# Normalisation and input projection merged into one stage, with the value differences formed in it

## What is computed

```python
h = layer_norm(x, ln0_g, ln0_b)
proj = jnp.einsum('btd,dc->btc', h, w_in[l])
qa, ka, va, qb, kb, vb, gate = jnp.split(proj, split_at, axis=-1)
ya = dilated_mixture(heads_a(qa), heads_a(ka), heads_a(va), rel_bias)
yb = stick_breaking(heads_b(qb), heads_b(kb), heads_b(vb))
y = jnp.concatenate([ya, yb], axis=-1) * jax.nn.silu(gate)
out = jnp.einsum('btc,cd->btd', y, w_out[l]) + b_out[l]
h = layer_norm(DEEPNORM_ALPHA * h + out, ln_g[l], ln_b[l])
```

## Time and profile before

| what | us |
|---|---|
| median of 3 runs | 2041.08 (2038.07 to 2041.69) |
| span of the profiled execution | 2037.5 |
| TensorE matmul busy | 1769.6 (87%) |
| VectorE busy | 1250.8 (61%) |
| ScalarE busy | 781.5 (38%) |
| GpSimd busy | 341.2 (17%) |

### The profile page before, as it was taken

How to read it: one execution, slowest core, us unless ns; L and a number is a source line. 1 busy time by engine, 2 the same in 40 slices (tenths; PEclk the granted TensorE clock), 3 DMA queues, 4 the chain that set the end, 5 groups by cost and what they waited for, 6 DMA issues and landing times. The chain is left out here.

```text
span 2037.5 us, 29563 instructions
## 1 busy us (share of the span) xinstructions
PE 1769.6 (87%) x9134; PEld 1473.7 (72%) x9134; DVE 1250.8 (61%) x2303; ACT 781.5 (38%) x1927; POOL 341.2 (17%) x222
## 2 busy tenths in 40 slices
PE   4688999999999999487887788788998999959886
PEld 3566888888887878365666566567998989947775
DVE  8402122121122321699999999995776676768998
ACT  5301111111110010365565565565886776830000
POOL 4100000000000000312212211310222222206554
PEclk8798999999999999789899999997999999969998
DMA  5396233331121431804413440435897978363331
GB/s 169 56 108 167 113 141 117 121 137 62 62 93 55 114 88 41 193 10 91 93 31 67 90 89 14 87 67 131 190 205 184 197 191 192 95 214 138 124 124 72
DMA packets 224187, 230.92 MB, mean 113 GB/s; under 512 B 126996, under 2 KB 187412, under 8 KB 215357
## 3 DMA queue, kind: packets, MB, share of 16 engines
q1 hardware_dynamic: 170540, 162.09, 31.9%
q10 hardware_dynamic: 51424, 62.93, 8.6%
q0 software_dynamic: 2112, 4.73, 3.3%
HBM read 145.03 MB, written 84.67 MB: 113 GB/s over the span
## 5 line engine op out<-in xcount | busy, mean ns | idle before, releaser
L411 PE MATMUL proj<-h_hi,w_hi 128*128 128x512 f32 x1024 | 403.3, 394 | 33.0 <-DVE w_lo L497 29.6
L411 PE MATMUL proj<-h_hi,w_lo 128*128 128x512 f32 x1024 | 400.6, 391 | 0.0
L411 PE MATMUL proj<-h_lo,w_hi 128*128 128x512 f32 x1024 | 400.2, 391 | 0.0
L805 PE MATMUL wt_ps<-ident,W 128*128 128x128 f32 x1088 | 189.3, 292 | 97.3 <-DVE WT_lo L908 95.4
L899 DVE TENSOR_TENSOR_SCAN W<-w,W,zeros 128x512 f32<-128x512 f32 x192 | 266.5, 1388 | 0.0
L805 PEld LDWEIGHTS wt_ps<-ident,W 128*128 128x128 f32 x1088 | 129.8, 146 | 179.7 <-DVE WT_lo L908 105.7
L858 ACT ACTIVATE WT_hi<-wt_ps 128x512 fp32r<-128x512 f32 (+1 forms) x320 | 171.0, 534 | 209.4 <-PE o_ps L825 205.3
L411 PEld LDWEIGHTS proj<-h_hi,w_hi 128*128 128x128 f32 x1024 | 193.5, 189 | 73.9 <-issue 34.6
L521 DVE TENSOR_TENSOR st_lo<-proj,st_hi 128x512 fp32r<-128x512 f32 x64 | 44.0, 691 | 299.7 <-ACT st_hi L469 250.8
L411 PEld LDWEIGHTS proj<-h_hi,w_lo 128*128 128x128 f32 x1024 | 193.2, 189 | 40.7
L411 PEld LDWEIGHTS proj<-h_lo,w_hi 128*128 128x128 f32 x1024 | 193.5, 189 | 39.7
(11 more groups left out here) (116 smaller groups left out, 3138.1 us busy)
## 6 DMA issues: line engine op xcount, KB each, us to landing
w_raw<-in_w_tiles SPq DMA_DIRECT2D x32, 512.0 KB, 3.4
qk_hi_d<-st_hi ACTq DMA_DIRECT2D x16, 1024.0 KB, 3.9
qk_lo_d<-st_lo ACTq DMA_DIRECT2D x16, 1024.0 KB, 6.8
va<-va_d SPq DMA_DIRECT2D x32, 512.0 KB, 10.6
moved<-move_d SPq DMA_DIRECT2D x16, 528.0 KB, 4.2
x_sb<-in_x SPq DMA_DIRECT2D x16, 512.0 KB, 3.7
gate_d<-st_lo ACTq DMA_DIRECT2D x8, 1024.0 KB, 3.9
q_hi<-qk_hi_d SPq DMA_DIRECT2D x16, 512.0 KB, 10.0
```

The costliest lines, as they stand in the source:

```text
L411: last = pe.matmul(acc[s % 4][:], w[j][:, k, :], h[:, k, cols], start=(n == 0), stop=(n == len(passes) - 1))
L805: last = pe.transpose(t_ps[n % 4][:, i * P:(i + 1) * P], W[(turn_index(u) + i) % W_SLOTS][:, j * P:(j + 1) * P], ident[:])
```

## The change

`norm_phase` and `projection_phase` become one block, `front_phase`. A "step" s is one column block k of one chunk g of 512 positions (s = 8g + k, 32 steps). In each step TensorE does the four transposes of step s + 2 and then 9 matmuls: the three products of block k for each of the first `LEAD` = 3 weight tiles. So the first 3 tiles (12 of the 128 groups) are projected while the rows are being normalised; the other 29 tiles (116 groups) follow as before. Further:

- x is normalised in place, in 8 slots. ScalarE writes gain and bias back into the transposes' PSUM bank (`ln_tp`), then copies the high part out; VectorE subtracts from the bank. `ln_tp` has two banks.
- The high part of the weights moves from VectorE to ScalarE (`high_w`); one `w_raw` buffer stands where there were two.
- Results are stored group by group (512 positions), from two staging tiles `st`, and SP issues the stores, between its loads.
- The three DMAs of the bias tables move from GpSimd to SP; their sources lie in `st`, so the first two results (`first(0)`, `first(1)`) wait for `toe_stored`.
- For values of B, ScalarE copies the result shifted by one column (`shifted`), VectorE subtracts before the transposes, and the differences are stored split, as `dv_d` (rows of 512 bytes for each head). The block ends are collected in `vend`, transposed once and stored as `vend_d`.
- In `stick_phase` the values' three loads become two, and `differences` is gone.
- The order of the weight tiles changes.

```diff
+    LEAD = 3
...
+    X_SLOTS, W_SLOTS, ST_SLOTS, ACC_SLOTS, T_SLOTS, V_SLOTS = 8, 3, 2, 4, 2, 2
+        @block.sync
...
+            for c in range(3):
+                sp.wait_ge(toe_out, c + 1)
+                src = st[c % 2][0:HEADS, (c // 2) * CH:(c // 2) * CH + TOE]
+                sp.dma_start(toe_d[c], src.unsqueeze(1).broadcast_to([HEADS, P, TOE])).then_inc(toe_stored, 16)
+            load_w(LEAD)
+            for g in range(1, NCH):
+                if g + 1 < NCH:
+                    for n in range(QB * (g + 1), QB * (g + 2)):
+                        load_x(n)
+                for n in range(LEAD * (g - 1), LEAD * g):
+                    store(n)
...
+        @block.tensor
...
+            for s in range(STEPS):
+                g, k = divmod(s, KD)
+                pe.wait_ge(lo_done, s + 1)
+                for t in range(LEAD):
+...
+                    products(n, k, k == KD - 1)
+                if s + T_SLOTS < STEPS:
+                    transposes(s + T_SLOTS)
...
+        @block.scalar
...
+            def first(n):
+                kind = KIND[n]
+                if n >= ST_SLOTS:
+                    act.wait_ge(st_stored[n % ST_SLOTS], stored_by(n - ST_SLOTS))
+                else:
+                    act.wait_ge(toe_stored, 16 * 3)
+...
+            for s in range(STEPS):
+                g, k = divmod(s, KD)
+                normed(s)
+                if s in (0, 1):
+                    high_w(s + 1)
...
+                if g > 0 and k == 0:
+                    for n in range(LEAD * (g - 1), LEAD * g):
+                        first(n)
+            high_w(LEAD)
...
+        @block.vector
...
+            for s in range(STEPS):
+                g, k = divmod(s, KD)
+                low_h(s)
+                if s in (0, 1):
+                    low_w(s + 1)
+                if g > 0 and k == 0:
+                    for n in range(LEAD * (g - 1), LEAD * g):
+                        second(n)
+                if g + 1 < NCH and k < QB:
+                    moments(QB * (g + 1) + k)
+                if g + 1 < NCH and 0 < k <= QB:
+                    normalise(QB * (g + 1) + k - 1)
-            pool.wait_ge(w_split, 2 + TILES)
-            for c in range(3):
-                pool.dma_start(toe_d[c], toe[:, c, :].unsqueeze(1).broadcast_to([HEADS, P, TOE])) \
-                    .then_inc(toe_stored, 16)
-            def differences(it, par):
-    ...
-                pool.tensor_tensor(v_diff[:], v_prev[par][:], v_cur[par][:], ALU.subtract).then_inc(dv_step, 1)
```

More of the change, by code:

```diff
@@ L156, in wait_high @@
[L156 to L168, removed]
+        full_done, hi_done, lo_done = m.sem("h_full_done"), m.sem("h_hi_done"), m.sem("h_lo_done")
@@ new lines, in _ @@
+            for n in range(4):
+                load_x(n)
+            load_w(0)
+            load_x(4)
+            load_x(5)
+            load_w(1)
+            load_x(6)
+            load_x(7)
+            load_w(2)
+            sp.wait_ge(rb_set, 2)
+            sp.dma_start(rb[0:N_BUCKETS, :], rel_bias).then_inc(rb_loaded, 16)
+            for c in range(3):
+                where = vt[c] if c < 2 else tin[0]
+                sp.dma_start(where[0:N_BUCKETS + 1, 0:TOE], onehot[:, c * TOE:(c + 1) * TOE]) \
+                    .then_inc(oh_loaded, 16)
@@ new lines, in _ @@
+            for n in range(LEAD * (NCH - 1), LEAD * NCH):
+                store(n)
+            for n in range(MAIN, len(GROUPS)):
+                t, ch = GROUPS[n]
+                if ch == 1 and t + 1 < W_TILES:
+                    load_w(t + 1)
+                if n > MAIN:
+                    store(n - 1)
+                if n == VB_LAST + 3:
+                    sp.wait_ge(vend_copied, 1)
+                    for a in range(2):
+                        sp.dma_start(vend_d[:, :, a, :],
+                                     vend_t[a * TB:(a + 1) * TB, :].rearrange("b (h d) -> b h d", h=HEADS)) \
+                            .then_inc(vend_stored, 16)
@@ L182, in _ @@
+            store(len(GROUPS) - 1)
+            for slot in range(ST_SLOTS):
+                sp.wait_ge(st_stored[slot], stored_by(len(GROUPS) - ST_SLOTS + slot))
+            sp.wait_ge(vend_stored, 16 * 2)
         @block.gpsimd
@@ L191, in _ @@
                 .then_inc(ident_step, 1)
-            pool.wait_ge(ident_step, 2)
-            def deviation(n):
+            for n in range(TB):
                 pool.wait_ge(mv_done, n + 1)
@@ L245, in _ @@
[L245 to L271, removed]
-                    for c in range(3):
-                        last = pe.matmul(toe_ps[c][0:HEADS, 0:TOE], rb[:], oh[:, c * TOE:(c + 1) * TOE],
-                                         start=True, stop=True)
-                    last.then_inc(toe_mm, 1)
@@ L277, in _ @@
[L277 to L303, removed]
@@ L549 @@
+            low_w(LEAD)
+            for n in range(LEAD * (NCH - 1), LEAD * NCH):
+                second(n)
+            for n in range(MAIN, len(GROUPS)):
+                t, ch = GROUPS[n]
+                if ch == 2 and t + 1 < W_TILES:
+                    low_w(t + 1)
+                if n in V_INDEX:
+                    out_of_acc(n)
+                if n - 1 in V_INDEX:
+                    second(n - 1)
+                if n not in V_INDEX:
+                    second(n)
 class HeadTiles:
```

566 lines of the change are left out of this document (285 added, 281 removed).

## The result

The changed kernel takes 2054.63 us in the median of 5 runs (2049.63 to 2057.91), the kernel before 2041.08 in 5 runs taken with them: a ratio of 1.0076, 95% interval 1.0057 to 1.0096. That is slower by 0.8%, more than the noise of the runs. The forecast was 2039, with faster as the likeliest outcome (0.41); the time lies inside the forecast range of 2005 to 2062, but on the side that got 0.31. The profiled execution spans 2050.1 us against 2037.5, so the profile has 12.6 of the 13.6 us to explain.

The account below looks back on a forecast made before the run. The prediction took TensorE to bound the projection from 200 us on and VectorE the stick phase. The stick phase starting 36.6 us later, less 38 gained, gave -1.4 on 2041.1: 2039.7, rounded to 2039; range 2005 to 2062.

Parts of the forecast that it names:

- the stick phase's gain: Stick phase without GpSimd's differences: 33.4 us from scans, 3 from the load, 1.5 from three scans at the start, sum 38.
- The rest of the merged part: From the tables' landing at 140 to the merged part's end at 208.7: 5 + 20.4 + 22.4 + 19.5 + 1.4 us.
- the chain-bound rival: Merged part's steps limited by the chain through two `ln_tp` banks: 3.5 us a step, +19, time 2058; chance 0.15.
- The stall: Merged part: TensorE stands still from 58 to 145, 87 us, while ScalarE's first results wait for the tables.
- The rival of quick tables: Tables on SP's queue done by about 70 us, the stall shrinking by 70, time 1969; chance 0.12.
- The rival of 28 GB/s: Eight engines carry the tables at 3.5 GB/s each, taking 169 us, 73 more, time 2112; chance 0.05.
- The 1.6 us of start: Start allowance for the tables' DMAs on SP's queue, in 42 + 1.6 + 96 = 140 for their landing.
- The prediction's own sign of being wrong: Merged part: the prediction is wrong if steps take over 2.9 us; it had 2.67 in the mean.
- The old stall: Kernel before, 100 to 150 us: TensorE's wait of 29.6 us in two pieces on the weights' split, said to go.
- check of 816.7: Kernel before: 74.7, TensorE's groups, transposes, 29.6 of wait and 2.6 of slow matmuls, against last transposes at 816.23.

Follow-up runs that it names:

- e3: Changed kernel with the third result copy and subtraction of each chunk moved three steps later: 2031.4 us, 0.9960 of the kernel before.
- e7: Changed kernel with tables computed on 128 partitions but stored from eight of them, 16 apart: 2004.2 us, 0.9836 of the kernel before.
- e8: Changed kernel with four copies of each head's row and tables stored from eight partitions, 4 apart: 1981.1 us, 0.9712 of the kernel before.
- e4: Changed kernel with tables computed on 128 partitions and stored from all 128: 1972.1 us, 0.9666 of the kernel before.
- e1: Changed kernel with bias tables staged in tiles only the value groups need, still on SP's queue: 2049.7 us, 1.0058 of the kernel before.
- e2: Changed kernel with bias tables staged in tiles only the value groups need and sent from GpSimd's queue: 2024.4 us, 0.9945 of the kernel before.
- b1: Kernel before, without value differences on GpSimd, values loaded straight into the operands: 1999.8 us, 0.9806 of the unedited kernel before.

## Why the prediction was off

The sum, term by term, in us:

| term | predicted | measured |
|---|---|---|
| the tables' DMAs are issued at | 42 | 41.0 |
| they land at | 140 | 137.7 |
| from there to the end of the merged part (224.4) | 68.7 | 86.7 (e3: 67.2) |
| from there to the start of the stick phase (875.7) | 651.3 | 651.3 |
| the stick phase's gain | 38 | 38.7 |
| change of the span | -1.4 | +12.6 |

**The step that failed** is "The rest of the merged part": 68.7 us predicted, 86.7 measured. It put the wait for a free slot of `st` at nothing there. It charged the three results with "three copies on ScalarE (0.6 each, overlapped to 1.5)" after the landing and with "one of 4.0 where the three results come in" in each chunk, as work alone. The third copy is not only work: it reuses the slot of the first, whose store has only just been issued. In the three places inside this stretch the wait took 7.5, 5.5 and 3.3 us, 16.3 in all, and TensorE came back from each at a lower clock, an estimated 3.3 us more than behind the long stall alone. e3 took these waits away, and the stretch came out at 67.2 (from the landing at 136.38 to 203.57), 1.5 under the prediction's 68.7. The fourth wait, 3.8, lies behind the stretch and costs TensorE little: it is busy 5.51 of the 6 us from 224 to 230. (The 68.7 has a slip of its own: 19.5 for chunk 3 is less than eight steps of its 2.55, 20.4.) The prediction did look at this buffer, and only in the long phase: "Stores of 256 or 512 KB a group have two groups, 10.9 us, until their staging tile is wanted." That holds for the 116 groups of 5.4 us and is confirmed there (651.3). In the merged part three results come at once, so the cover is not two groups but none.

That the time still lies in the range is luck. The range reached up to 2062 for the sake of the chain-bound rival, whose 2058 is nearer to 2054.6 than my own number, but for a reason that did not hold (below).

**The stall was right, and so was its size.** The tables moved at 50 GB/s from SP's queue as from GpSimd's, and landed 2.3 us before the forecast. The source was the limit: e7 shows it by changing only where the eight partitions lie (51 to 103 GB/s), and e8 and e4 fit (202 and 364). The rival of quick tables (0.12) was wrong: 0.51 MB in 10 us from SP's queue in e1, 0.50 from GpSimd's in e2. The rival of 28 GB/s was wrong too, since half the engines (a share of 0.44) carried 50. The prediction put the stall down to `first(0)`'s wait alone and let the queue matter only for x and the weights; e1 shows that the place in the queue makes the stall without that wait, by the store behind the tables. The 1.6 us of start in the sum stand in no row and no run shows them; from the issue at 41.0 to the landing at 137.7 are 96.7 us, and 4.73 MB at 50 GB/s leave some 2 of them.

**Steps.** The prediction's own sign of being wrong, steps over 2.9 in the merged part, came true in the mean: 23 steps took 86.7 - 5 - 1.4 = 80.3 us, 3.5 each. That is the chain-bound rival's figure, but the rival did not hold: a step without moments takes 2.52 where TensorE's own work was put at 2.55, and in e3 the low parts of steps with moments start at 163.11, 165.78 and 168.49, 2.7 apart, the 2.72 that the prediction took from the earlier trace rows. The mean is made of such steps and three waits.

**The old stall.** The prediction said "the old stall of 29.6 goes". 18.6 was there to go. Its check of 816.7 counted the 11.03 twice, since 74.7 already held it, so the check agreed by accident: without it the sum is 805.7, 10.5 short. The trace of the kernel before places most of these: TensorE is idle for 5.0 us between 600 and 816, where the value groups are; it does 29 matmuls in 8.59 busy us from 160 to 170, at a clock of 0.73, some 2 us more than at full clock; and a group takes 5.44 us (22 of them between the copies at 500.92 and 620.60), not 5.42. The forecast does not use that sum, so its number is not touched.

**Stick phase.** 33.4 for the scans beside GpSimd and up to 2.4 for the three at the start; b1 has 36.4 for all of them, the changed kernel 36.8. 38 in all against 38.7. Without the differences the scans' median stays (1.267 and 1.268) and only the long ones go. These runs show that the differences cause the stretch, not by what means. In the pair of rows that the prediction shows, the excess (3.44 - 0.68 = 2.76) is longer than the whole `v_diff` instruction (2.36); it fits only with the gate product that GpSimd runs just ahead of it (L755, 941.52 to 942.84), from the scan's start at 942.28 to the end of L736 at 945.17.

## What to carry to other kernels

When an asynchronous store reads from a ring of staging tiles, count for each stage how many results come in a burst and how long the store holds a slot: two slots were ample for one result in 5.4 us and cost 19.5 us where three came together, in front of an engine that had other work behind the copy. The small table that a DMA repeats many times out of eight neighbouring partitions moved at 50 GB/s on either queue here, out of eight that lie 4 apart at 202, and out of all 128 at 364: compute such a table on more partitions, or on partitions that lie 4 apart. What it cost came from what the start of the kernel needed and found behind it in one queue (in e1 one wait of 90.6 us), so look at what is queued behind it before merging stages around it.

## What the runs showed of the hardware that I had not expected

The same transfer of the tables holds 94% of the engines' time from GpSimd's queue (e2) and 45% from SP's (e1), at the same 0.50 MB in 10 us. In e2 the three DMAs are issued within 5 us, in e1 they take 41 us to issue; and in the kernel before the share on GpSimd's queue falls to 47.8% towards the end. So part of the difference may be how many of the three are in flight at once, which no run separates from the queue. In e2 a store of 256 KB next to it takes SP 7 us to issue. From SP's queue the issuing instructions themselves stand, in the changed kernel's timeline: 42 us for the three tables, then 31 for a weight tile and 18 for four tiles of x:

```profile
41.04 41.99 SPq L250 DMA_DIRECT2D toe_d<-st  x3
83.08 31.31 SPq L209 DMA_DIRECT2D w_raw<-in_w_tiles  x1
114.44 17.73 SPq L203 DMA_DIRECT2D x_sb<-in_x  x4
```

So in these 91 us behind the slow transfer it was the engine that stood, not only its data, and whatever else that engine was to issue.
